# Where the weight sums of a seven-product SwiGLU are formed: VectorE in place of GpSimd in the gate and up half

## The reference

```python
h = layer_norm(ALPHA * x + mixed @ w_out, ln_mix_g, ln_mix_b)
f = (jax.nn.silu(h @ w_ffn_gate) * (h @ w_ffn_up)) @ w_ffn_down
return layer_norm(ALPHA * h + f, ln_ffn_g, ln_ffn_b)
```

## Time and profile before

| what | us |
|---|---|
| median of 2 runs | 2844.11 |
| the two runs | 2838.22 and 2850.0 |
| the profiled execution's own time | 2844.51 |
| its span, first to last instruction | 2842.9 |

### The profile page before, as it was taken

The page is one execution under the profiler, slowest core; times in us unless marked ns, Lnnn a source line. Parts: engine busy times, 40 slices in busy tenths (PEclk is TensorE's granted clock), DMA queues, the critical chain, the costliest instruction groups (busy, mean ns, idle before and its releaser), DMA issues.

```text
span 2842.9 us, 51406 instructions
## 1 busy us (share of the span) xinstructions
PE 2595.6 (91%) x18345; PEld 2502.5 (88%) x18345; DVE 1578.3 (56%) x2325; ACT 976.2 (34%) x1444; POOL 1828.3 (64%) x2044
## 2 busy tenths in 40 slices
PE   6999999999999994799999999999999899999982
PEld 5999999998878894799999899999989799999982
DVE  6334343434665456655555555555555666777776
ACT  4222222223443223434343333434333432333332
POOL 4102020202431178999999999999999887777784
PEclk9999999999999997899999999999999999999996
DMA  5223231322222221343343434334343376555522
GB/s 165 79 66 118 61 120 57 117 72 79 57 55 72 69 76 63 97 133 121 110 146 115 139 118 138 115 117 140 113 143 115 131 214 194 180 177 181 183 68 96
DMA packets 286336, 327.78 MB, mean 115 GB/s; under 512 B 15872, under 2 KB 272336, under 8 KB 279648
## 3 DMA queue, kind: packets, MB, share of 16 engines
q1 hardware_dynamic: 270096, 208.72, 24.8%
q10 hardware_dynamic: 6448, 87.43, 8.3%
q0 software_dynamic: 9664, 29.80, 3.7%
HBM read 265.00 MB, written 61.34 MB: 115 GB/s over the span
## 4 chain that ended last, share of the span: by engine, by line
POOL 47%; PE 35%; issue 8%; DVE 6%; ACT 2%; DMA 1%; POOLq 1%; ACTq 0%; DVEq 0%; SPq 0%
PE G L624 18%; POOL zr L2142 15%; POOL zr L2140 12%; POOL zr L2144 11%; PE G L640 7%; PE G L1005 2%; PE A L733 2%; POOL fz L2173 1%; PE A L1005 1%; POOL fz L2181 1%; PE A L753 1%; POOL fz L2178 1%; DMA zr<-in_w_ffn_down 1%; ACT lg L1231 1%; POOL sg L2173 1%
## 5 line engine op out<-in xcount | busy, mean ns | idle before, releaser
L1806 DVE TENSOR_TENSOR zl<-zr,zh 128x896 fp32r<-128x896 f32 x528 | 647.4, 1235 | 602.2 <-ACT zh L1354 591.9
L1354 ACT CAST zh<-zr 128x896 fp32r<-128x896 f32 x528 | 499.3, 946 | 882.7 <-POOL zr L2144 772.1
L1005 PE MATMUL G<-hq,zh 128*128 128x288 f32 x2816 | 604.3, 308 | 112.9 <-ACT s L1384 50.5
L1005 PEld LDWEIGHTS G<-hq,zh 128*128 128x128 f32 x2816 | 467.6, 196 | 127.3 <-ACT s L1384 55.3
L2142 POOL TENSOR_TENSOR zr<-zr 128x256 f32<-128x256 f32 x528 | 475.6, 901 | 41.4
L2144 POOL TENSOR_TENSOR zr<-zr 128x128 f32<-128x128 f32 x528 | 442.2, 837 | 41.4
L1005 PE MATMUL A<-hq,zh 128*128 128x288 f32 x2112 | 442.6, 301 | 0.0
L1005 PE MATMUL G<-hq,zl 128*128 128x288 f32 x1408 | 428.2, 304 | 0.0
L2140 POOL TENSOR_TENSOR zr<-zr 128x128 f32<-128x128 f32 x528 | 373.8, 708 | 78.3 <-DMA zr<-in_w_ffn_down 78.2
L1482 DVE TENSOR_TENSOR wl<-raw,wh 128x512 fp32r<-128x512 f32 x200 | 165.0, 829 | 461.8 <-ACT wh L1103 461.5
L1005 PEld LDWEIGHTS A<-hq,zh 128*128 128x128 f32 x2112 | 352.9, 196 | 0.4
(11 more groups left out here) (304 smaller groups left out, 4229.7 us busy)
## 6 DMA issues: line engine op xcount, KB each, us to landing
zr<-in_w_ffn_gate SPq DMA_DIRECT2D x176, 256.0 KB, 2.8
zr<-in_w_ffn_up SPq DMA_DIRECT2D x176, 256.0 KB, 2.8
zr<-in_w_ffn_down SPq DMA_DIRECT2D x176, 256.0 KB, 3.0
raw<-in_w_in SPq DMA_DIRECT2D x168, 256.0 KB, 2.9
f_kept<-fq ACTq DMA_DIRECT2D x20, 2016.0 KB, 7.5
ring_a<-f_kept ACTq DMA_DIRECT2D x11, 2016.0 KB, 8.7
ring_b<-f_kept ACTq DMA_DIRECT2D x9, 2016.0 KB, 8.4
raw<-in_w_out SPq DMA_DIRECT2D x64, 256.0 KB, 2.7
```

The source lines that it names most:

```text
L1005: mm = pe.matmul(pbank(m), w[:, slot, W_OF[m], :], x[:, half, X_OF[m], :], start=first and one, stop=last and w is zl)
L1354: act.copy(zh[:, slot], zr[:, slot, 0:7, :]).then_inc(z_hi, 1)
L1806: dve.tensor_tensor(zl[:, slot], zr[:, slot, 0:7, :], f32(zh[:, slot]), ALU.subtract).then_inc(z_lo, 1)
```

## The change

`z_sum`, the same three instructions, is now also defined on DVE. DVE forms the sums of the pieces 0 to 355: those of the normalisation's 8 steps, of all 22 pairs, and the first four of the down half that belong to the last steps of the pairs' loop. At each step it stands ahead of `z_low`. POOL keeps `centre`, `h_sum`, `both`, `f_sum`, and the weight sums of the rest of the down half; before these it waits until DVE has made its last sum. Nothing is computed otherwise.

```diff
             def z_low(n, slot):
...
+            def z_sum(n, slot, landed):
+
+                q = zr[:, slot]
+                dve.wait_ge(z_in[slot], landed)
+                dve.tensor_tensor(q[:, 3, :], q[:, 7, :], q[:, 6, :], ALU.subtract).then_inc(z_diff, 1)
+                dve.wait_ge(z_diff, n + 1)
+                dve.tensor_tensor(q[:, 0:2, :], q[:, 3:8:4, :], q[:, 5:6, :].to_broadcast([P, 2, P]), ALU.add).then_inc(z_sums, 1)
+                dve.wait_ge(z_sums, n + 1)
+                dve.tensor_tensor(q[:, 2, :], q[:, 4, :], q[:, 0, :], ALU.subtract).then_inc(z_ready, 1)
...
             c.link(dve.reciprocal(rstd[:, :], rstd[:, :]))
+            z_sum(0, 0, 16)
...
                 if j + 2 < KS:
                     centre(j + 2)
+                z_sum(j + 1, (j + 1) % Z_SLOTS, (j + 1) // Z_SLOTS * 16 + 16)
                 z_low(j, j % Z_SLOTS)
...
                     if not first or t >= 5:
+                        z_sum(i * (2 * KS) + (t + 4), t % Z_SLOTS, i * 64 + ((t + 4) // Z_SLOTS * 16 + 16))
                         z_low(i * (2 * KS) + (t + 3), (t + 3) % Z_SLOTS)
...
             centre(1)
-            z_sum(0, 0, 16)
             centre(2)
             for j in range(KS):
                 h_sum(j)
                 if j + 3 < KS:
                     centre(j + 3)
-                z_sum(j + 1, (j + 1) % Z_SLOTS, (j + 1) // Z_SLOTS * 16 + 16)
...
                 for t in range(2 * KS):
-                    if not first or t >= 5:
-                        z_sum(i * (2 * KS) + (t + 4), t % Z_SLOTS, i * 64 + ((t + 4) // Z_SLOTS * 16 + 16))
...
+            pool.wait_ge(z_ready, N_FIRST + 4)
             for mp in range(8):
```

## The result

The median fell from 2844.11 to 2768.7 us (two runs, 2767.65 and 2769.76), a ratio of 0.9736 with a 95% interval of 0.970 to 0.9771. Five more runs of the same kernel beside nine of the kernel before gave 2759.06 and a ratio of 0.9718 [0.970, 0.9735]. The profiled execution took 2767.65 us, its span 2766.1. The forecast was 2762.

What follows compares the result with a forecast made beforehand. POOL's weight sums were taken to bound the gate and up half; 21 x (4.77 - 1.1) = 77 us in the pairs plus 5 in the normalisation, 82 off 2844.5, gave 2762 us, range 2735 to 2813.

Steps and rivals of the forecast that it cites:

- What bounds the kernel: Gate and up half: POOL 95 per cent busy; PE loses 4.77 us a pair around the gate-to-up boundary, 100 us at most.
- The sums on DVE: In the pairs, one piece's three sums cost DVE 0.98 us, bounds 0.77 and 1.77; a `z_low` costs 1.03.
- POOL's turns: Ahead of the gate block's `combine`, one `both` and three `f_sum` instructions cost DVE 1.1 + 1.1 + 0.5 + 0.5 = 3.2 us.
- the rival at 2787: In the pairs, POOL's turns cost DVE their full length, 4.4 us in place of 3.2, 25 in all; chance 0.05.
- The place of the loss: At the gate block's end, `combine` starts at T + 23.35, and PE waits 1.0 us for its first instruction.
- T: The end of the pair before, where the next gate block starts; 1300.3 in the trace of the kernel before.
- The other banks: After `combine`'s first instruction, the other banks follow at up to 0.49 us against PE's 0.40, 0.1 more loss.
- The cover: Between T and `combine` nothing else is late; DVE's new wait for a piece's DMA costs nothing, with 1.2 us cover.
- The clock: Behind the boundary's new stop of about 1.0 us, no clock fall; a fall costs 1.7 us a pair, rival's chance 0.2.
- The normalisation: In the normalisation's 8 steps, some 0.8 us a step saved, less 1.0 for the first sum: 5 us, bounds 0 and 12.
- starved turns: In the pairs, POOL gets no turn until DVE rests, loss 6.9 us a pair against 4.77: 2884 us, chance 0.05.
- dear sums: In the pairs, a piece's sums cost DVE far more than 0.98 us; from 1.23 nothing is gained; chance 0.05.

Runs made afterwards that it cites:

- the move that gives 1.2 us a pair: `f_low` from step 4 to 10, its store from 6 to 13: in the changed kernel 2745.51 us, in the kernel before 2850.04 us.
- `all_dve`: The changed kernel with POOL's `both` and `f_sum` of the pair loop also on DVE: 2749.41 us, ratio 0.9672 to the kernel before.
- `f_low_twice`: The changed kernel with `f_low` done twice at step 4, the same result written twice: 2837.85 us, ratio 0.9986 to the kernel before.

## Why the prediction was right

The forecast of 2762 lies 6.7 us under the first median, 2.9 over the second one. By its own steps:

- **What bounds the kernel.** POOL's sums set the pace. Shown from both sides: the move that gives 1.2 us a pair after the change gives nothing before it, and DVE making a quarter of the sums already gave four fifths of the gain.
- **The sums on DVE.** 0.98 us a piece and 1.03 a `z_low` were forecast from other DVE instructions. A step without disturbance takes 1289.23 - 1287.24 = 1.99, of which 1.00 is `z_low`. The chained starts, 0.03 to 0.04 behind each end, are as taken.
- **POOL's turns.** 3.2 were forecast. The sums beside `both` and `f_sum` lasted 1.56, 1.56, 0.78 and 0.89 in place of 0.42, 0.42, 0.29 and 0.28: 1.14 + 1.14 + 0.49 + 0.61 = 3.38. The full lengths, the rival at 2787, would have been 4.4. `all_dve` confirms the price by removing it. The Trainium skill ("SBUF — State Buffer", section "SBUF: two separate sides") says that the lock is held for the whole instruction and that the loser is blocked. The traces agree that the two take turns; they also show that DVE loses somewhat less than the length of POOL's instruction, 1.14 of 1.43 and 0.49 and 0.61 of 0.81.
- **The place of the loss.** The forecast put `combine` 23.12 us behind the start of the up block's last `combine` instruction (T + 23.35 against T + 0.23); it started 1306.88 - 1283.75 = 23.13 behind it. PE's stop was put at 1.0, and is 1.03. That the first of these fits to 0.01 is partly luck: POOL's turns were 0.18 longer than forecast, and eight steps of 1.99 in place of 2.01 were 0.16 shorter.
- **The other banks.** Here a term was too small: 0.1 forecast, 0.25 measured. This is why the period is 46.04 and not 45.9: 3 us in 21 pairs.
- **The cover.** In the pairs nothing else was late, and DVE waited for no piece's DMA.
- **The clock.** It stays at 1.00 behind all 22 stops, of 0.85 to 1.15 us idle. In `f_low_twice` it fell at 18 of 21 boundaries.
- **The normalisation.** 5 us forecast, 3.2 and 3.0 measured. The term that was too large is "some 0.8 a step is saved": it took POOL's list as the step's only limit. It measured 0.6, because DVE's list, at 9.61 of 9.68 us, now fills the step and POOL waits for rows that come from DVE by way of ACT.

Sum: 73.9 + 3.2 = 77.1 measured in these two stretches, 82 forecast; how near the medians come to 2762 depends by several us on the stretches outside. The rivals that named a worse price for POOL's turns, starved turns or dear sums fall with the rows above: POOL's `both` starts 0.08 us behind the end of the `combine` instruction that it waits for (1284.29 against 1283.75 + 0.46), and a piece's sums cost 1.0 us. One sign that the prediction had named as wrong did come up: `f_sum` ends at 1296.85, T + 13.3, later than T + 13. It does no harm, as `f_low`, at 1300.73, has no wait in front of it.

## What to carry to other kernels

An engine that is 95 per cent busy ahead of the bound is worth relieving, but the new owner's list has to be laid out between its own deadlines: the same instructions in another order gave 1.2 us a pair more here, and one extra 2.3 us instruction ahead of the deadline took 3.6 away. Two engines that take turns at SBUF pay for each other's instructions, so count the slower one's work at the faster one's price too. Busy time is not an engine's list: waits that stand in its order ahead of other work belong to it.

## What was not expected of the hardware

- VectorE got faster by doing GpSimd's additions itself: a 576-column addition costs it 0.67 us when it makes it and 1.14 when GpSimd makes it beside it.
- A GpSimd sum of 0.46 us lasts up to 2.47 us when it stands behind a 2016-column subtraction of VectorE, so that one turn costs GpSimd 2.0 us.
- Two stops of PE of some 1.5 and 1.4 us, 0.6 us of work apart, were followed by nearly 6 us at a granted clock of about 0.5 at one boundary and by none at another with the same stops. Single stops of about 1 us were followed by none at all 22 boundaries.
